# A two-layer hybrid decoder step on one core: seven value chunks of the first four sequences move among the last key tiles

## The reference

```
z = rmsnorm(x) @ w_in                      # u | q | k | v | two gates of 1024 columns
for each of 3 head groups (window, dilation) = (128,1), (512,4), (2048,16):
    scores = q . [cached keys, new keys] * 64**-0.5 - slope * distance      # 8 heads of 64
    out, lse = softmax(scores) . [cached values, new values]
a_att = mix of the 3 groups by their denominators
x += (sigmoid(g_pool) * (a_pool @ P_pool) + sigmoid(g_att) * (a_att @ P_att)) @ w_out
x += FFN(rmsnorm(x))                       # dense in layer 0, top-2 of 8 experts in layer 1
```

## Time and profile before

| | us |
|---|---|
| median of 3 runs | 2021.56 |
| lowest and highest | 2020.85, 2023.05 |
| the profiled execution, its own time | 2023.46 |
| its span | 2021.6 |
| PE busy in it | 1937.9 |
| DVE, ACT, POOL busy | 611.7, 491.1, 146.6 |

### The profile page before, as it was taken

How to read it: one execution, slowest core, us unless ns; L and a number is a source line. 1 busy time by engine, 2 the same in 40 slices (tenths; PEclk the granted TensorE clock), 3 DMA queues, 4 the chain that set the end, 5 groups by cost and what they waited for, 6 DMA issues and landing times.

```text
span 2021.6 us, 45327 instructions
## 1 busy us (share of the span) xinstructions
PE 1937.9 (96%) x20758; PEld 1333.6 (66%) x20759; DVE 611.7 (30%) x1022; ACT 491.1 (24%) x756; POOL 146.6 (7%) x214
## 2 busy tenths in 40 slices
PE   6998988989998999998899999999999999999998
PEld 5998866989998998886785353544435353444535
DVE  4455632554435455651442101010111001010101
ACT  3434432444334443541331000000000000000000
POOL 0113100102211011300010000000000000000000
PEclk9999999999999999999999999999999999999999
DMA  7543688745545344488834999999999999999996
GB/s 231 166 132 118 211 278 305 241 131 162 163 162 180 128 146 141 140 281 288 294 131 145 385 393 371 389 376 389 366 393 389 372 396 370 389 369 396 373 386 255
DMA packets 211728, 552.66 MB, mean 273 GB/s; under 512 B 11362, under 2 KB 107658, under 8 KB 195008
## 3 DMA queue, kind: packets, MB, share of 16 engines
q1 hardware_dynamic: 207184, 541.67, 73.9%
q0 software_dynamic: 3072, 8.00, 1.1%
q10 hardware_dynamic: 1280, 0.06, 0.1%
HBM read 542.28 MB, written 7.76 MB: 272 GB/s over the span
## 4 chain that ended last, share of the span: by engine, by line
PE 90%; DVE 3%; DMA 3%; ACT 2%; issue 1%; POOL 0%; DVEq 0%; SPq 0%; ACTq 0%; POOLq 0%
PE psum L900 84%; PE psum L908 6%; DMA low_part<-in_w_in 3%; ACT w_split L1476 1%; DVE w_split L1754 1%; DMA high_part<-in_const_a 0%; DVE high_part L1765 0%; DVE xn_split L1769 0%; DVE high_part L1761 0%; DVE low_part L1747 0%; ACT low_part L1511 0%; DVE low_part L2197 0%; ACT high_part L1453 0%; DVE low_part L1848 0%; DVE high_part L1853 0%
## 5 line engine op out<-in xcount | busy, mean ns | idle before, releaser
L900 PE MATMUL psum<-low_part 128*32 128x512 f32 (+3 forms) x6926 | 678.9, 528 | 12.0 <-ACT low_part L1449 5.6
L900 PE MATMUL psum<-xn_split,w_split 128*128 128x288 f32 x3744 | 529.1, 302 | 37.3 <-DVE w_split L1754 18.1
L900 PEld LDWEIGHTS psum<-xn_split,w_split 128*128 128x128 f32 x3744 | 515.0, 193 | 61.9 <-DVE w_split L1754 30.1
L900 PEld LDWEIGHTS psum<-low_part 128*32 128x32 f32 (+2 forms) x6926 | 243.0, 115 | 403.6 <-issue 390.7
L1754 DVE TENSOR_TENSOR w_split<-low_part,w_split 128x2048 fp32r<-128x2048 f32 x105 | 240.9, 2295 | 390.3 <-ACT w_split L1476 390.3
L900 PE MATMUL psum<-low_part,high_part 128*32 128x256 f32 (+3 forms) x6636 | 346.2, 360 | 3.7 <-DVE low_part L1747 2.7
L900 PEld LDWEIGHTS psum<-low_part,high_part 128*32 128x32 f32 (+1 forms) x6636 | 217.7, 111 | 129.1 <-issue 16.2
L1476 ACT ACTIVATE w_split<-low_part 128x2048 fp32r<-128x2048 f32 x105 | 201.0, 1914 | 372.3 <-PE psum L900 236.7
L908 PE MATMUL psum<-high_part,low_part 128*128 128x128 f32 (+3 forms) x1004 | 131.2, 281 | 13.0 <-DMA high_part<-in_const_a 10.0
L1449 ACT ACTIVATE high_part<-psum 128x384 f32<-128x384 f32 (+2 forms) x72 | 32.4, 498 | 442.0 <-PE psum L908 410.5
L908 PEld LDWEIGHTS psum<-high_part,low_part 128*128 128x128 f32 (+3 forms) x1004 | 111.3, 142 | 34.4 <-issue 20.0
(11 more groups left out here) (147 smaller groups left out, 944.7 us busy)
## 6 DMA issues: line engine op xcount, KB each, us to landing
low_part<-in_we_down SPq DMA_DIRECT2D x112, 1024.0 KB, 7.8
low_part<-in_cache_kv_g SPq DMA_DIRECT2D x72, 1024.0 KB, 5.5
low_part<-in_we_gate SPq DMA_DIRECT2D x64, 1024.0 KB, 8.2
low_part<-in_we_up SPq DMA_DIRECT2D x64, 1024.0 KB, 7.3
low_part<-in_w_in SPq DMA_DIRECT2D x56, 1024.0 KB, 5.2
low_part<-in_we_gate SPq DMA_DIRECT2D x64, 768.0 KB, 6.5
low_part<-in_we_up SPq DMA_DIRECT2D x64, 768.0 KB, 6.4
low_part<-in_w_dense SPq DMA_DIRECT2D x33, 1024.0 KB, 5.2
```

Source lines behind the costliest of these rows:

```text
L900: signal(e.matmul(out, lhsT, rhs, start=start, stop=stop, skip_group_check=mixed), inc)
```

## The change

- `VALUES_BEHIND` puts V0 behind the tiles of K4, V1 and V2 behind K5, V3 and V4 behind K6, V5 and V6 behind K7. Both the transfers (`CACHE_LIST`) and PE (`values_after`) follow this order: K4 V0 K5 V1 V2 K6 V3 V4 K7 V5 V6 K8 G0.
- `V_BEHIND` becomes `(2, 1, 1, 2, 2, 2, 1, 0)`: V7, V8 behind G0, V9 behind G1, V10 behind G2, and so on.
- `EX0_GATE` goes from 4 to 1: the first half's result is gathered behind G1.
- G0 is split behind the last key tiles (ACT after tile 70, DVE after tile 71), and ACT copies every even tile, DVE every odd one, to the end.

```diff
-V_BEHIND = (2, 3, 3, 3, 3, 2, 2, 0)
+VALUES_BEHIND = (0, 0, 0, 0, 1, 2, 2, 2, 0)
+V_BEHIND = (2, 1, 1, 2, 2, 2, 1, 0)
 def value_steps():
-    out, v = [], 0
+    out, v = [], sum(VALUES_BEHIND)
...
+def cache_list():
+
+    out, v = [(0, 0, q) for q in range(NQ)], 0
+    for q, n in enumerate(VALUES_BEHIND):
+        out.append((0, 1, q))
+        out += [(1, 0, v + i) for i in range(n)]
+        v += n
+    return out + [(1, 0, q) for q in range(v, NQ)] + [(1, 1, q) for q in range(NQ)]
...
+def values_after(m):
+
+    q, last = divmod(m - NT, BH)
+    if not (0 <= q < NQ and last == BH - 1):
+        return []
+    return [sum(VALUES_BEHIND[:q]) + i for i in range(VALUES_BEHIND[q])]
...
 def copied_by_act(m):
 
-    left = HB * NT - m
-    return left in (8, 7, 6, 5, 4, 2) or left > 11 and m % 2 == 0
+    return m % 2 == 0
...
-EX0_GATE = 4
+EX0_GATE = 1
...
-                for m in range(REST, HB * NT + LAG):
-                    cache_step(m)
...
+                for m in range(REST, HB * NT + LAG):
+                    cache_step(m)
+                    for v in values_after(m):
+                        cache_values(v)
...
-                    if m == HB * NT - 11:
+                    if m == HB * NT - 2:
                         split_high(L, W_MERGE)
...
-                    if m == HB * NT - 8:
+                    if m == HB * NT - 1:
                         split_low(L, W_MERGE)
```

More of the change, by code:

```diff
@@ L128, in chunk_kinds @@
     steps = ["W" if kind == "G" else "C" for kind, _ in V_STEPS]
-    return ["W"] * N_IN + ["C"] * (N_CACHE // 2) + steps + ["W"] * (KT + N_DENSE)
+    return ["W"] * N_IN + ["C"] * (N_CACHE // 2 + sum(VALUES_BEHIND)) + steps + ["W"] * (KT + N_DENSE)
 class Tally:
@@ L183 @@
 NQ = NT // BH
+def cache_list():
[5 more added lines that the diff above has]
+    return out + [(1, 0, q) for q in range(v, NQ)] + [(1, 1, q) for q in range(NQ)]
+CACHE_LIST = cache_list()
+def values_after(m):
[3 more added lines that the diff above has]
+    return [sum(VALUES_BEHIND[:q]) + i for i in range(VALUES_BEHIND[q])]
 CACHE_SLOTS = 8
 def copied_by_act(m):
-    left = HB * NT - m
-    return left in (8, 7, 6, 5, 4, 2) or left > 11 and m % 2 == 0
+    return m % 2 == 0
 FIRST_STEP = 2
@@ L365 @@
 CACHE_ORDER = {c: n for n, c in enumerate(c for c, kind in enumerate(KINDS) if kind == "C")}
-CACHE_CHUNK = list(CACHE_ORDER)
+CACHE_CHUNK = {CACHE_LIST[n]: c for c, n in CACHE_ORDER.items()}
 W_MERGE, W_BRANCH, W_OUT, W_UP, W_DOWN = N_IN, N_IN + KT, N_IN + 3 * KT // 2, NW_ATT, NW_ATT + N_UP
@@ L791, in send_cache @@
                 def send_cache(c):
-                    kv, half, n = CACHE_ORDER[c] // (HB * NQ), CACHE_ORDER[c] // NQ % HB, CACHE_ORDER[c] % NQ
+                    kv, half, n = CACHE_LIST[CACHE_ORDER[c]]
                     b0 = half * BH
@@ L800, in send_cache @@
                     send(L, c, [(view(slot(c), BH, 512), src)])
-                for c in range(C_CACHE, C_CACHE + N_CACHE // 2):
+                for c in range(C_CACHE, C_CACHE + N_CACHE // 2 + sum(VALUES_BEHIND)):
                     send_cache(c)
-                c = C_CACHE + N_CACHE // 2
+                c = C_CACHE + N_CACHE // 2 + sum(VALUES_BEHIND)
                 for kind, n in V_STEPS:
@@ L1090, in cache_tile @@
                     where, i, g, b, t = TILES[n]
-                    c = CACHE_CHUNK[(HB * kv + half) * NQ + where]
+                    c = CACHE_CHUNK[kv, half, where]
                     if n == 0 or TILES[n - 1][0] != where:
```

## The result

The changed kernel is slower by 0.4%: 2032.47 us in the median of 9 executions (2026.14 to 2035.65) against 2023.05 us of the kernel before (9 executions), a ratio of 1.0042 (95% interval 1.0031 to 1.0053). Once more, on another occasion and with 12 executions, the ratio was 1.0016 (1.0000 to 1.0032), so the size of the loss is less sure than its sign. The forecast was 6.0 us less, a ratio of 0.997. The profiled execution has a span of 2033.1 us, 11.5 us more than before.

What follows compares the result with a forecast made beforehand. PE was taken to hold 90% of the chain of waits, nearly all the rest being waits for weight chunks. Gains of 2.5 (layer 0) and 3.5 us (layer 1) gave 2021.56 - 6.0 = 2015.6 us; own range 2011 to 2019, wider 2008 to 2023.

Steps and rivals of the forecast that it cites:

- Step (2): Key tiles up to G0's landing: queue full behind V3, 3.1 us per megabyte, six megabytes, G0 lands at 289.9 us.
- Step (4): Before G0: its split becomes visible, PE idles 3.4 us, G0 starts at 294.2 and low clock costs 1.5 us.
- Step (5): From G0 to the branch projections: PE has 68.3 us of work, ending at 364.0 with no further wait.
- Step (6): Gates: only G5 and G6 still wait, 1.2 us each, clock stays up; layer 0 ends at 366.4, 2.5 us less.
- Step (1): Around V0: a value chunk costs PE 0.93 us, new tokens' values 2.8 us, a place's next issue comes 1.0 us later.
- Step (3): Up to the last scores: PE's own work is 22.4 us, ending at 284.2, so no bound.
- the rival of the spread clock: Pieces from V3 to K8 all run at 1.2 GHz, costing 3.0 us per layer: 2021.6 us, no change; chance 0.25.
- Step (7): Gathering behind G1 moves its copy behind G3's split: taken as nothing, at most 0.3 us either way.
- slow mixed transfers: Alternating value and key chunks transfer slowly: over 0.2% slower from 3.93 us per megabyte, 2027.6 us at 4.1; chance 0.15.

Runs made afterwards that it cites:

- small_values: Changed kernel with the seven moved value chunks loaded with 16 of their 128 partitions, PE's work unchanged: 2020.56 us, ratio 0.9981 to the kernel before.
- small_repaired: Changed kernel with EX0_GATE = 4, V_BEHIND = (2, 2, 2, 2, 1, 1, 1, 0) and 16 of 128 partitions loaded of V0 to V6: 2012.42 us, ratio 0.9949.
- early_places: Changed kernel with a 4-column matmul behind each value group among the keys, ahead of each gate, giving ring places back at once: 2030.27 us, ratio 1.0038.
- kept_busy: Changed kernel with two unused 512-column matmuls at each of five PE waits, before V4, K7, V6, K8 and G0: 2025.62 us, ratio 1.0010.
- gates_reordered: Changed kernel with V_BEHIND = (2, 2, 2, 2, 1, 1, 1, 0), fewer values behind G4 and G5: 2023.99 us, ratio 1.0000 to the kernel before.
- the two late repairs: Changed kernel with EX0_GATE back at 4 (0.9998), or V_BEHIND = (2, 2, 2, 2, 1, 1, 1, 0) (1.0000); both together 2022.71 us, ratio 1.0002.

## Why the prediction was wrong

The direction was wrong. The mechanism that was to bring the gain is there: G2, G3 and G4 no longer wait, and the gates' waits fell from 10.4 us to 3.4 in layer 0 and from 11.5 (the prediction took 10.4 for both layers) to 3.8 in layer 1. What failed are the terms on the other side: G0's landing and start, steps (2) and (4), and, behind it, steps (5) and (6). (2), (4) and (5) took PE's pieces at full clock, (2) took the queue as full from V3 on, and (6) let a transfer behind two others land as fast as one alone. In layer 0 the branch projections came 10.6 us later than forecast, in layer 1 5.4 us.

- **Step (1) and the shared order up to K4** held in layer 1: V1 with V2 take 1.92 us, the new tokens' values with V0 3.83. In layer 0 the common point moved by 0.6 us, and V0 took 4.51 us with K5's first transposes at 1.97, together 1.6 us more than forecast, at the low clock and without a wait. The prediction priced neither.
- **Step (2), G0's landing, failed**: 32.9 us behind the common point in layer 0 and 31.4 in layer 1, where 30.15 was forecast. Its sentence that behind V3 "the queue stays full" does not hold: V4 goes into K5's place, and K5 is transposed only behind V0 and its 2.8 us of new tokens' values, so ahead of V4's landing the DMA share was 0.76. V4's transfer was issued at 271.82 and landed at 277.16; by (2), moved by the common point's 0.6 us, V4 was due at 275.0. Of these 2.2 us 1.6 are the low clock at V0 and K5; in layer 1, where it stayed up, V4 landed 15.3 us behind the common point, 0.7 us late. From there to K8's landing at 290.24 four transfers landed 3.27 us apart, not 3.1, which is 0.7 us (3.29 us in layer 1). That the bytes delay G0 is shown by small_values and small_repaired; that late places do, beyond half a microsecond, is not (early_places). The 358 GB/s that the Trainium skill gives for one core ("DMA: Bandwidth & Descriptors", Specifications) would have made the landing earlier still; the stretch from 277 to 300 us moved 366 GB/s, which is more. Landings 3.27 us apart are 321 GB/s; the rest went into transfers that landed later.
- **Step (3) held** as far as small_values shows it: without the bytes G0 starts at 31.5. Less 2.41 us of wait for the split, 0.94 for the copy and 3.29 for K7 that leaves 24.8 us of PE's work, 24.5 by (3). In the changed kernel's layer 0 the same work took some 4 us more at the low clock.
- **Step (4) was right in kind and too small.** The split is visible and G0 takes 7.93 us (8.1 forecast). But ACT's high part waited until 295.75 for the copy of tile 70, because K8's transposes and scores ran at the low clock. From K8's landing to G0's start it was 9.8 us, 7.6 in layer 1 and 7.4 by (4). So G0 started at 39.7 and not 34.4 behind the common point. This was the rival of the spread clock, in layer 0; in layer 1 K7 had it, K8 not, G0 started at 36.1 and then took 9.03 us. The rule of the Trainium skill on such stretches ("TensorE: Matmul & The Clock Gate", HAM oscillation) was weighed as a rival at 2021.6 us; the trace agrees with it only in part: K8 behind its wait ran at the low clock, K7 and V6 behind theirs of 2.37 and 2.80 us did not, and the mean from 277 to 300 us was 0.84. As a cost, kept_busy limits it: with the clock restored the median fell by 0.8 us, within the intervals.
- **Step (5), the work from G0 on, failed in layer 0 by 3.1 us.** V9 with G2 took 13.6 us in place of 10.5, at the low clock without a wait. I took the clock to fall only after idle time. In layer 1 it stayed up, in both profiles of the changed kernel. Moving EX0_GATE put narrow work next to narrow work and made the spell more likely (8 of 14 layers against 2 of 18).
- **Step (6) was right for G5** (1.02 and 0.97 us; 1.2 forecast) **and wrong for G6**: 2.38 and 2.80 us, and then 8.1 us of low clock. I let G6's transfer land 5.3 us after its issue; it took 7.58 us (349.23 to 356.81 in the chain) since V15 and V16, issued with G5, still filled the queue. That is 2.6 us in layer 0 and 3.1 in layer 1. gates_reordered removes the wait.
- **Step (7)** changed nothing that shows.

The terms for layer 0: G0's start 5.3 (1.6 the clock at V0 and K5, 2.2 the clock at K8, 1.5 transfers and the rest), G0 itself -0.2, V9 and G2 3.1, G5 -0.2, G6 2.6, together 10.6. For layer 1: 1.6 (1.4 K8's landing, 0.2 the rest), 0.9, 0, -0.2 and 3.1, together 5.4. Both sums are those of one profiled execution on the slow side of the kernel's spread; the medians moved by 9.4 us at first and by 2.5 us beside the experiments.

The rival that had the sign right, slow mixed transfers, had the wrong reason: it needed 3.93 us or more for a megabyte, and landings came 3.27 us apart.

As a whole, the late split alone costs 0.4 to 0.5%, on the kernel before, and the seven megabytes cost 6 to 10 us. Against both stands what the emptier gates give, and seven is more than the key tiles can carry; five is not. Two things stay open: why the two late repairs don't add up in the median (0.9998, 1.0000, together 1.0002), and why early_places, with little low clock ahead of G0, isn't faster. The spells at V0, K8 and V9 come and go between executions, layers and kernels, and one profile of each kernel does not tell how often.

## What to carry to other kernels

When transfers are moved forward in a ring, follow each place on its own, the neighbours' too, up to the first weight chunk that must be split: its landing is the new start of everything. Move as many as fit beside the work that is there (here one value chunk for each key chunk), not as many as relieve the other end. And a wait of PE should be priced with its clock: the wait of 2.4 us ahead of G0 cost 1.3 to 2.5 us more in 16 of the 19 layers that show it, and nothing more in three. Lastly, before a difference between two profiles is given to an edit, the same records should be compared for their clock: the 4.4 us by which early_places starts G0 earlier look like its edit and are two spells of low clock.

## What the hardware showed that I had not expected

The granted clock fell while PE was busy. In layer 0 of the changed kernel 0.96 us of 16-column matmuls followed by 2.8 us over 32 rows left V9 and G2 at 5.24 and 8.36 us in place of 3.83 and 6.66; the same 32-row matmuls at V0, with no 16-column work near, left 4.51 and 1.97 us in place of 3.83 and 1.09. The same columns over 128 rows did neither (none of 4 stretches; over 32 rows 12 of 26 at V0 and 10 of 32 at V9). The stretch of V9, and that of G2, in the changed kernel's layer 0 (columns as in the earlier trace rows):

```profile
311.00:322.90 11.90, 11.90 (x68) 8.01 (x66) 3.44 (x3) 2.73 (x3) 0.00 (x0) 0.88 0.80 266
322.90:331.30 8.40, 8.40 (x56) 8.16 (x54) 1.45 (x2) 0.41 (x1) 0.00 (x0) 0.77 0.78 249
```

PE is busy without a gap in both, at 0.88 and 0.77.

The mean clock also differs from one execution to the next, so that one profile is a poor witness of a few microseconds: twelve executions of the changed kernel lay 15 us apart, and the one at a mean clock of 0.988 took 12 us less than the one at 0.977.
